# The setup of a hybrid diffusion step in another order: x first, eight condition slots, root by columns

## The reference

```python
mod_ctx = jax.nn.silu(c_ctx[None, :]) @ w_ada[l] + b_ada[l]
mod_lat = jax.nn.silu(c) @ w_ada[l] + b_ada[l]
...
sh1, sc1, g1, sh2, sc2, g2 = jnp.split(mod[:, None, :].astype(dt), 6, axis=-1)
h = rmsnorm(x, n1) * (1 + sc1) + sh1
u = h @ w_in
...
h = jnp.sin(freq * (feats @ fw1.astype(f32) + fb1.astype(f32)))
h = jnp.sin(freq * (h @ fw2.astype(f32) + fb2.astype(f32)))
```

## Time and profile before

| | |
|---|---|
| median of 3 runs | 2668.11 us (2666.4 to 2668.53) |
| profiled execution, its own time | 2663.65 us |
| its span | 2661.7 us |
| busy: TensorE / VectorE / ScalarE / GpSimd | 94% / 55% / 22% / 26% |
| setup, up to the last matmul of projection tile 0 | 0 to 110 us |
| one pass of the first loop | 42.8 us |

### The profile page before, as it was taken

The page is one execution under the profiler, slowest core; times in us unless marked ns, Lnnn a source line. Parts: engine busy times, 40 slices in busy tenths (PEclk is TensorE's granted clock), DMA queues, the critical chain, the costliest instruction groups (busy, mean ns, idle before and its releaser), DMA issues.

```text
span 2661.7 us, 34768 instructions
## 1 busy us (share of the span) xinstructions
PE 2491.2 (94%) x13438; PEld 2100.7 (79%) x13438; DVE 1474.5 (55%) x2723; ACT 590.5 (22%) x857; POOL 681.5 (26%) x300
## 2 busy tenths in 40 slices
PE   5599999999997999999899989799999999999995
PEld 2388888867776888888778878588888888888884
DVE  6878786566585776677754453752233322333227
ACT  3222222564654222222220011210000000000002
POOL 0211111211211232223223433423133231332310
PEclk9699999999998999999999999899999999999997
DMA  6144443212124232223363232101011010110102
GB/s 257 68 165 159 171 163 122 75 39 79 39 65 161 98 115 97 97 97 114 118 219 126 91 105 85 56 32 40 23 47 47 32 39 24 47 47 32 39 8 79
DMA packets 53536, 234.04 MB, mean 88 GB/s; under 512 B 6052, under 2 KB 8548, under 8 KB 47861
## 3 DMA queue, kind: packets, MB, share of 16 engines
q1 hardware_dynamic: 53492, 233.47, 24.6%
HBM read 178.91 MB, written 54.53 MB: 88 GB/s over the span
## 4 chain that ended last, share of the span: by engine, by line
PE 45%; DVE 4%; issue 1%; DMA 0%; ACT 0%; DVEq 0%; ACTq 0%
PE ps L772 15%; PE ps L773 15%; PE ps L774 15%; DVE h_lo L1746 1%; DVE x L1863 1%; DVE x L1742 0%; DVE z_lo L1731 0%; DVE ps L1861 0%; DVE h_lo L1503 0%; DVE zraw L1776 0%; DVE w_raw L1827 0%; DVE side L1499 0%; DVE side L1739 0%; DMA zraw<-scratch_za_s 0%; DMA zraw<-scratch_zb_s 0%
## 5 line engine op out<-in xcount | busy, mean ns | idle before, releaser
L772 PE MATMUL ps<-h_hi,w_hi 128*128 128x512 f32 (+1 forms) x2256 | 816.8, 362 | 41.8 <-DVE h_lo L1503 17.1
L773 PE MATMUL ps<-h_lo,w_hi 128*128 128x512 f32 (+1 forms) x2256 | 803.8, 356 | 0.0
L774 PE MATMUL ps<-h_hi,w_lo 128*128 128x512 f32 (+1 forms) x2256 | 803.5, 356 | 0.0
L733 POOL TENSOR_TENSOR w_hi<-w_raw,zero_col 128x1024 fp32r<-128x1024 f32 x102 | 214.8, 2106 | 1680.5 <-PE ps L774 1245.3
L772 PEld LDWEIGHTS ps<-h_hi,w_hi 128*128 128x128 f32 x2256 | 429.2, 190 | 116.6 <-issue 29.0
L774 PEld LDWEIGHTS ps<-h_hi,w_lo 128*128 128x128 f32 x2256 | 429.7, 190 | 61.6
L773 PEld LDWEIGHTS ps<-h_lo,w_hi 128*128 128x128 f32 x2256 | 430.1, 191 | 59.3
L1811 DVE TENSOR_TENSOR a<-sil,ps 128x512 f32<-128x512 f32 (+1 forms) x66 | 39.5, 599 | 508.0 <-PE ps L774 506.9
L736 POOL TENSOR_TENSOR w_lo<-w_raw,w_hi 128x1024 fp32r<-128x1024 f32 x102 | 275.1, 2697 | 8.0
L1845 DVE SCALAR_TENSOR_TENSOR x<-ps,mod,x 128x512 f32<-128x512 f32 (+1 forms) x264 | 172.1, 661 | 96.1 <-PE ps L774 95.5
L1366 ACT ACTIVATE sil<-ps 128x512 f32<-128x512 f32 (+1 forms) x66 | 34.7, 527 | 764.0 <-PE ps L774 764.0
(11 more groups left out here) (244 smaller groups left out, 3407.7 us busy)
## 6 DMA issues: line engine op xcount, KB each, us to landing
w_raw<-in_weights SPq DMA_DIRECT2D x146, 512.0 KB, 3.8
ada_w<-in_w_ada SPq DMA_DIRECT2D x20, 1024.0 KB, 7.2
scratch_gate_s<-g_st SPq DMA_DIRECT2D x24, 640.0 KB, 3.3
side<-scratch_gate_s SPq DMA_DIRECT2D x24, 640.0 KB, 3.9
scratch_k_s<-kstage SPq DMA_DIRECT2D x8, 1536.0 KB, 6.6
hy_k<-scratch_k_s SPq DMA_DIRECT2D x8, 1536.0 KB, 8.6
scratch_hy_s<-hout SPq DMA_DIRECT2D x16, 640.0 KB, 3.2
x_in<-in_x SPq DMA_DIRECT2D x8, 640.0 KB, 9.2
```

Source lines behind the costliest of these rows:

```text
L733: nc.gpsimd.tensor_tensor(hi[:], w_raw[slot % 2][:], zero_col[:].to_broadcast([P, D]), ALU.add).then_inc(pool_step, 1)
L772: mm(out, w_pair[0], x_pair[0], start=first, stop=False)
L773: mm(out, w_pair[0], x_pair[1], start=False, stop=False)
L774: return mm(out, w_pair[1], x_pair[0], start=False, stop=last)
```

## The change

What the diff does, in the setup:

- SyncE loads all of x right behind the filter net's operands, then `vec` and `ident`, then eight condition slots, the two weight tiles and `fwd`, with no wait. Six of the slots (`ada_early`) and the angle work lie in memory of `h_hi` and `h_lo`, which is not written yet. Slots 8 and 9 follow when the first row has been taken.
- ScalarE takes the filter layers out of PSUM with scale and bias (`take_filter`), squares into two buffers, and makes one sine per layer. VectorE reduces a whole layer's angle at once, with two steps of `TWO_PI` in place of three.
- The sums of squares become columns on TensorE (ten matmuls of two columns, `SQUARES_UNIT`); root and reciprocal are then taken of [128, 20]. A diagonal matrix per 128 tokens, `rstd_diag`, and `ones` spread the result into `ps[0..2]`.
- Conditions come in four units of two slots, turn r right behind row r.
- Piece 0 of x is multiplied by the root in place, between the units. Its normalization is then one scalar operation on VectorE into `u_t`, while ScalarE rounds from `x_in` with scale and bias. Pieces 1 and 2 read the root in PSUM.
- Softplus stands behind the last remainder.

```diff
-TWO_PI = [6.28125, 0.0019350051879882812, 3.0199e-07]
+TWO_PI = [6.28125, 0.0019353071795864769]
...
+            sp.dma_start(x_in[:, 0, :], dr["x"][0]).then_inc(x_loaded[0], 16)
             sp.dma_start(cvec[:], dr["cvec"]).then_inc(cvec_in, 16)
-            sp.dma_start(ident[:], dr["ident"]).then_inc(consts_in, 16)
+            for k in range(1, KD):
+                sp.dma_start(x_in[:, k, :], dr["x"][k]).then_inc(x_loaded[k], 16)
             sp.dma_start(vec[:], dr["vec"]).then_inc(vec_in, 16)
...
-            for g in range(4):
-                sp.dma_start(ada_w[g][:], dr["w_ada"][g]).then_inc(ada_in[g], 16)
-                load_x(((0,), (1,), (2,), (3, 4))[g])
-            for g in range(4, ADA_FIRST + 2):
-
-                sp.wait_ge(ada_row_ready, g - 3)
...
+            for g in range(ADA_FIRST):
                 sp.dma_start(ada_w[g][:], dr["w_ada"][g]).then_inc(ada_in[g], 16)
+            load_tile(0, 0)
+            load_tile(1, 1)
+            sp.dma_start(fwd[:], dr["fwd"]).then_inc(consts_in, 16)
+            sp.wait_ge(ada_row_ready, 1)
...
+            pe.wait_ge(x_sq_summed, KD - 1)
+            for tile in range(NT):
+                ins = mm(out[:, 2 * tile:2 * tile + 2], x_sq_sum[:, tile * P:(tile + 1) * P], ones[:, 0:2],
+                         start=True, stop=True)
...
+            for r in range(ROWS_FIRST):
+                ada_row_unit(u_setup, 0, ROW_UNIT[r], [2 * r, 2 * r + 1], 16)
+                ada_turn_unit(u_setup, 0, TURN_UNIT[r], r + 1, 0, 512)
+                if r == 0:
+
+                    pe.wait_ge(diag_ready, 1)
                     for b, (a, e, _) in enumerate(PIECES):
-                        mm(ps[b][:, 0:e - a], ones[:], x_sq_sum[:, a:e],
+                        mm(ps[b][:, 0:e - a], ones[:],
+                           rstd_diag[:, a // P:e // P, :].rearrange("p t m -> p (t m)"),
                            start=True, stop=True).then_inc(proj_done[b], 1)
...
+            for k in range(KD):
+                act.wait_ge(x_loaded[k], 16)
+                if k >= 3:
+
+                    act.wait_ge(x_sq_summed, k - 2)
+                fn((x_sq[k % 2] if k else x_sq_sum)[:], x_in[:, k, :], ACT.Square).then_inc(sq_ready, 1)
+                if k == 1:
+                    take_filter(0)
+                if k == KD - 3:
+                    act.wait_ge(arg_ready, 1)
+                    fn(h1f[:, :], arg[0:FILT_HID, :], ACT.Sin).then_inc(sin_ready, 1)
+            take_filter(1)
...
+                        fn(h_hi[:, k, a:e], x_in[:, k, a:e], ACT.Identity, bias=mod[:, k, seq:seq + 1],
+                           scale=norm_a[:, k, seq:seq + 1]).then_inc(hi_ready, 1)
...
+            sum_square(1)
+            reduce_angle(0)
+            for k in range(2, KD):
+                sum_square(k)
+            reduce_angle(1)
+
+            dve.wait_ge(rms_ready, 1)
+            own(nc.vector.reciprocal(rstd_col[:, :], rstd_col[:, :]))
...
+                for k in ((0, 1, 2), (3, 4, 5), (6, 7), ())[r]:
+                    dve.wait_ge(x_loaded[k], 16)
+                    own.add(tt(x_in[:, k, 0:512], x_in[:, k, 0:512], ps[0], ALU.mult))
...
+                            ts(u_t[n % 2][:, 0:e - a], x_in[:, k, a:e], norm_a[:, k, seq:seq + 1],
+                               mod[:, k, seq:seq + 1], ALU.mult, ALU.add).then_inc(u_ready, 1)
...
             dve.wait_ge(h_ready, 3 * KD)
+            softplus()
             own.restart()
```

More of the change, by code:

```diff
@@ L294, in build_program @@
         w_lo = [sb(ctx, f"w_lo{s}", [P, D], F32R) for s in range(2)]
+        st = ExitStack()
+        ada_early = [sb(st, f"ada_early{s}", [P, KD * 256]) for s in range(2, ADA_FIRST)]
+        feats = sb(st, "feats", [FILT_EMB, T])
+        h1f = sb(st, "h1f", [FILT_HID, T])
+        arg, turns = sb(st, "arg", [P, T]), sb(st, "turns", [P, T])
+        st.close()
         h_hi = sb(ctx, "h_hi", [P, KD, T], F32R)
@@ L321, in build_program @@
         ident = sb(fwd_stack, "ident", [P, P])
-        fwd_flat = fwd[:, :, :, :].rearrange("p q m f -> p (q m f)")
-        ada_w += [fwd_flat[:, s * KD * 256:(s + 1) * KD * 256] for s in range(2)]
+        ada_w += ada_early
         st = ExitStack()
@@ L328, in build_program @@
         x_sq_sum = sb(st, "x_sq_sum", [P, T])
[L329 to L330 removed]
+        x_sq = [sb(st, f"x_sq{s}", [P, T]) for s in range(2)]
+        f_bias = sb(st, "f_bias", [P, 2])
+        u_t = [sb(st, f"u_t{s}", [P, 512]) for s in range(2)]
+        rstd_col = sb(st, "rstd_col", [P, 2 * NT])
+        rstd_diag = sb(st, "rstd_diag", [P, NT, P])
         f_vec = sb(st, "f_vec", [P, 3])
@@ L1104, in _, with take_filter @@
             fn(csilu[:, :, 0:2], cvec[:], ACT.Silu).then_inc(csilu_set, 1)
-            def take_row(g):
-                src, free = take_mix(u_setup, 0, ROW_UNIT[g])
-                if g > 1:
-                    act.wait_ge(mod_ready, g - 1)
-                own(fn(ada_row[:, g % 2 * 256:g % 2 * 256 + 256], src[:, 0:256], ACT.Copy))
+            def take_filter(layer):
+                rows = P if layer else FILT_HID
+                if layer:
+                    act.wait_ge(sin_ready, 1)
+                act.wait_ge(f_bias_set, 1)
+                for j, (a, e, _) in enumerate(PIECES):
+                    src, free = take_mix(u_setup, 0, FILT_UNIT[3 * layer + j])
+                    fn(arg[0:rows, a:e], src[0:rows, 0:e - a], ACT.Identity, bias=f_bias[0:rows, layer:layer + 1],
+                       scale=f_vec[0:rows, 2:3]).then_inc(free, 1)
@@ L1112, in take_row @@
+            act.wait_ge(consts_set, 3)
+            src, free = take_mix(u_setup, 0, SQUARES_UNIT)
+            own(fn(rstd_col[:, :], src[:, 0:2 * NT], ACT.Sqrt, bias=eps[:, 0:1], scale=1.0 / D))
+            act.sem_inc(free, 1)
+            act.sem_inc(rms_ready, 1)
+            for r in range(ROWS_FIRST):
+                src, free = take_mix(u_setup, 0, ROW_UNIT[r])
+                act.wait_ge(mod_ready, r)
+                own(fn(ada_row[:, :], src[:, :], ACT.Copy))
                 act.sem_inc(free, 1)
```

194 lines of the change are left out of this document (90 added, 104 removed).

## The result

The changed kernel takes 2642.28 us (median, 2639.12 to 2642.6). Runs of the kernel before beside it gave 2667.26 (2664.45 to 2668.53). The ratio is 0.9906, with an interval of 0.9891 to 0.9922: 25 us faster. Its profiled execution took 2642.14 us, with a span of 2640.4 against 2661.7 before, which is 21.3 shorter. Why the medians differ by more than the profiled executions is told at the end of the prediction's points.

What follows compares the result with a forecast made beforehand. TensorE bounds the loop, a dependent chain with VectorE longest the setup. The last h_lo at 89.5 instead of 108.5 us gives -19.0, loop loads and softplus cost nothing; from the 2668.1 median the forecast is 2649 us, range 2639 to 2657.

Runs made afterwards that it cites:

- the gap of 64 bytes: Changed kernel with an unused 36-byte SBUF tile that shifts all tiles behind it by 64 bytes; 2638.07 us, ratio 0.9897.
- two loads: Changed kernel with extra one-element Exp and square root on ScalarE at each loop pass's head, so two table loads ahead of h_out's activation; 2629.44 us, ratio 0.9871.
- three loads: Changed kernel with extra one-element Exp, square root and sine at each pass's head, so three table loads ahead of h_out's activation; 2638.73 us, ratio 0.9895.
- the long reciprocal: Changed kernel with an unread VectorE reciprocal over 1280 columns put back ahead of the small one; 2652.14 us, ratio 0.9947.
- the early softplus: Changed kernel with softplus moved behind the first row and w3 and decay loaded before the last h_lo; 2644.64 us, ratio 0.9922.

## What to carry to other kernels

Ask of each GpSimd operation on SBUF which VectorE operations it will lie beside, since moving it only helps where VectorE idles or reads PSUM: of the places tried for the weight split here, only the change's own was such a one. Chains of small matmuls with evictions between them are cheaper in fewer, longer units, for the gaps and for the clock. And when a stage that an edit doesn't touch changes its time, compare where its tiles lie before looking for a cause in the edit.

## What the runs showed of the hardware

- **Addresses.** A shift of all later SBUF tiles by 32 bytes made a stage of back-to-back fp32r matmuls 1.0% faster (869.36 to 860.44 us, the same in four kernels); a shift by 64 gained 0.3% (866.74).
- **Shared access of VectorE and GpSimd.** Beside the split, VectorE's products, sums and scalar operations with all tensor operands in SBUF lasted about until the split's operation ended, with one tensor operand or two and however small: [128 x 16] took 2.2 us instead of 0.17. The reciprocal was not held up: 8.14 us over 1280 columns with a whole operation of the split beside it, which took its usual 1.89. Operations that read PSUM weren't either (`x_in` by `ps`, 0.63 us each in the changed kernel). The split is slowed too: its first operation took 3.15 us beside the angle work and 1.89 in the changed kernel.
- **The start of TensorE's fast stretch.** It isn't tied to a place in the program. TensorE works from 25.5 us on with gaps of under 1 us; the same row 0 and broadcast took 3.64 and 4.61 us in the changed kernel but 3.64 and 2.40 with the gap of 64 bytes, and 3.27 and 2.40 with two loads. The rows that follow are 3.75 us earlier in both (45.84 against 49.59 for row 2). Five of the twelve traces of the changed kernel and its variants have the early start (turn 0 in 1.02 us): these two, three loads, the long reciprocal and the early softplus. In none of the five do TensorE's instructions up to there, or what they wait for, differ from the changed kernel's; three have shifted tiles, and two don't. The four times of the kernel with the gap of 64 bytes fall into 2636.1, 2636.5 and 2639.7, 2640.5, which would fit; only one of each kernel's executions was profiled, so it isn't shown.
